# Encoder block on one core: the scan's 32x32 inversion split by column parity, its transfers merged and reordered, and the softmax weights computed ahead of the last row's norm

## The reference

```
def step(state, inp):
    r_t, w_t, k_t, v_t, kk_t, a_t = inp
    sa = einsum('zbhvk,zbhk->zbhv', state, -kk_t)
    state = (state * w_t[..., None, :] + sa[..., :, None] * (kk_t * a_t)[..., None, :]
             + v_t[..., :, None] * k_t[..., None, :])
    y = einsum('zbhvk,zbhk->zbhv', state, r_t)
...
kk = to_heads(k_raw * k_k);  kk = kk / max(sqrt(sum(kk * kk)), L2_EPS)
alpha = jax.nn.softmax(jnp.stack(lses), axis=0)        # weights of the three attention groups
o_attn = jnp.sum(alpha[..., None] * jnp.stack(outs), axis=0)
```

## Time and profile before

| | |
|---|---|
| median of 3 runs | 3364.0 us (3359.9 to 3370.8) |
| the profiled execution | 3362.9 us, span 3361.1 us |
| PE busy | 3258.0 us (97%) |
| DVE, ACT, POOL busy | 1852.6, 1310.0, 1580.3 us |
| projection / scan / output, from the span's start | 0 to 901.7 / to about 1600 / to 3361.1 us |

### The profile page before, as it was taken

How to read it: one execution, slowest core, us unless ns; L and a number is a source line. 1 busy time by engine, 2 the same in 40 slices (tenths; PEclk the granted TensorE clock), 3 DMA queues, 4 the chain that set the end, 5 groups by cost and what they waited for, 6 DMA issues and landing times.

```text
span 3361.1 us, 42103 instructions
## 1 busy us (share of the span) xinstructions
PE 3258.0 (97%) x15943; PEld 2692.0 (80%) x15943; DVE 1852.6 (55%) x2360; ACT 1310.0 (39%) x2139; POOL 1580.3 (47%) x1492
## 2 busy tenths in 40 slices
PE   7999999999889999999899999999999999999998
PEld 6788887777578888888588878888888888888886
DVE  3666565666667676772531034455455455455556
ACT  4544345554255665662442232223233233223222
POOL 4544443334278888885564443323323323323323
PEclk9999999999899999999899999999999999999999
DMA  5444454443455555552633323323323323323323
GB/s 171 122 151 138 141 154 132 129 120 103 114 137 143 129 130 141 146 135 82 242 115 136 113 69 113 107 88 107 112 83 109 111 81 117 103 84 117 107 82 106
DMA packets 666051, 405.06 MB, mean 121 GB/s; under 512 B 193534, under 2 KB 597178, under 8 KB 665338
## 3 DMA queue, kind: packets, MB, share of 16 engines
q1 hardware_dynamic: 665850, 402.38, 41.1%
HBM read 347.05 MB, written 54.53 MB: 119 GB/s over the span
## 4 chain that ended last, share of the span: by engine, by line
PE 50%; DVE 1%; ACT 0%; issue 0%; POOL 0%; DMA 0%; SPq 0%; DVEq 0%; ACTq 0%; POOLq 0%
PE f_bank L2207 9%; PE f_bank L2209 9%; PE f_bank L2208 9%; PE f_bank L2245 4%; PE f_bank L2247 4%; PE f_bank L2246 4%; PE f_bank L2185 2%; PE f_bank L2186 2%; PE f_bank L2187 2%; PE f_bank L2128 1%; PE f_bank L2129 1%; PE f_bank L2130 1%; PE f_bank L2163 0%; DMA orw_plain<-oat 0%; DVE orw_plain L2701 0%
## 5 line engine op out<-in xcount | busy, mean ns | idle before, releaser
L2496 POOL TENSOR_TENSOR w_lo_b<-w_raw_b,w_hi_b 128x1024 fp32r<-128x1024 f32 x176 | 435.9, 2479 | 903.4 <-ACT w_hi_b L2372 898.1
L2207 PE MATMUL f_bank<-act_rounded,w_lo_b 128*128 128x512 f32 x1408 | 549.2, 390 | 1.2 <-DVE act_rounded L2608 1.2
L2209 PE MATMUL f_bank<-act_rounded,w_hi_b 128*128 128x512 f32 x1408 | 547.8, 389 | 0.0
L2208 PE MATMUL f_bank<-act_rounded,w_hi_b 128*128 128x512 f32 x1408 | 547.8, 389 | 0.0
L1295 POOL TENSOR_TENSOR ring_w_rounded<-ring_w_plain,ring_w_hi 128x1024 fp32r<-128x1024 f32 x134 | 330.3, 2470 | 427.5 <-ACT ring_w_hi L1311 427.5
L1635 PE MATMUL slab_ps<-h_hi,ring_w_rounded 128*128 128x512 f32 x1056 | 426.4, 404 | 2.8 <-DVE h_lo L1462 2.4
L1636 PE MATMUL slab_ps<-h_lo,ring_w_hi 128*128 128x512 f32 x1056 | 414.9, 393 | 0.0
L1637 PE MATMUL slab_ps<-h_hi,ring_w_hi 128*128 128x512 f32 x1056 | 414.2, 392 | 0.0
L2372 ACT CAST w_hi_b<-w_raw_b 128x1024 fp32r<-128x1024 f32 x176 | 185.1, 1053 | 449.6 <-DMA w_raw_b<-in_w_ffn_up_dram 203.9
L2207 PEld LDWEIGHTS f_bank<-act_rounded,w_lo_b 128*128 128x128 f32 x1408 | 264.5, 188 | 55.7 <-DVE act_rounded L2608 1.1
L2209 PEld LDWEIGHTS f_bank<-act_rounded,w_hi_b 128*128 128x128 f32 x1408 | 264.3, 188 | 55.2
(11 more groups left out here) (434 smaller groups left out, 6176.9 us busy)
## 6 DMA issues: line engine op xcount, KB each, us to landing
ring_w_plain<-in_w_in_dram SPq DMA_DIRECT2D x190, 512.0 KB, 4.1
w_raw_b<-in_w_ffn_gate_dram SPq DMA_DIRECT2D x88, 512.0 KB, 3.6
w_raw_b<-in_w_ffn_up_dram SPq DMA_DIRECT2D x88, 512.0 KB, 3.6
w_raw_b<-in_w_ffn_down_dram SPq DMA_DIRECT2D x42, 512.0 KB, 3.9
w_raw_b<-in_w_out_dram SPq DMA_DIRECT2D x16, 1024.0 KB, 5.0
zt<-slab_out SPq DMA_DIRECT2D x63, 256.0 KB, 4.3
hid_plain<-in_w_ffn_down_dram SPq DMA_DIRECT2D x21, 512.0 KB, 4.2
oa_plain<-in_w_ffn_down_dram SPq DMA_DIRECT2D x21, 512.0 KB, 3.8
```

The lines of the kernel that those rows point to most:

```text
L2207: pe.matmul(o, wl[:, k, :], act_hi[:, kk, :], start=kk == 0, stop=False)
L2208: pe.matmul(o, wh[:, k, :], act_lo[:, kk, :], start=False, stop=False)
L2209: return pe.matmul(o, wh[:, k, :], act_hi[:, kk, :], start=False, stop=stop)
L2496: pool.tensor_tensor(low(r), slab_raw(j % 2), high(r).bitcast(F32), ALU.subtract).then_inc(slab_low, 1)
```

## The change

- *Inversion.* The inverse is no longer made in place but in a second tile, inv, of half the columns: each block goes to two partitions, 32 apart, and partition group r holds the columns of the inverse with parity r. Rows and columns of n on the side of a are stored with the even ones first and then the odd ones ("placed", "in_blocks"), so that POOL's operations still have regular strides. There are 31 steps of two operations, with 2k x n elements on 64 partitions. Three small masks are built at the start of the scan for the permuted orders.
- *ab and ak become abk.* Products with 64 rows of contraction, for each head of a group by itself, into two banks; no block-diagonal b_bd and k_bd, so ACT's "bd" goes. a comes to PE by way of var, and ACT negates it in "at". DVE masks in four stages' worth of 64-partition operations: "n" (the part that is stored) ahead of "ab" and "ak".
- *Transfers.* zt's rows are laid out so that six loads of a unit become two, and five of a bonus two. yb leaves in two stores, one for each parity, and blocks come in four loads of twice the partitions.
- *SP's order.* In odd slots the wait for the inversion and the yb stores stand first, then the n store, d_bd and low of the next unit, then the loads of blocks. d_bd and low of the other unit move to the next slot.
- *Projection.* "unit" of the last row moves from step TAIL + 2, ahead of "share", to step TAIL + 3, behind the first six "weigh"; its store moves with it.

```diff
-PE_SLOT = (("x1", "u"), ("ab", "v"), ("lx", "u"), ("ak", "v"), ("x3", "u"), ("av", "v"), ("qg", "u"),
+PE_SLOT = (("x1", "u"), ("abk", "v"), ("lx", "u"), ("x3", "u"), ("av", "v"), ("qg", "u"),
-DVE_SLOT = (("ab", "v"), ("xadd", "u"), ("ak", "v"), ("decays", "w"), ...
+DVE_SLOT = (("n", "v"), ("xadd", "u"), ("ab", "v"), ("ak", "v"), ("decays", "w"), ...
...
                 for it in range(NUNIT // 2):
-                    m = blocks[it % 2]
-                    pool.wait_ge(n_landed[it % 2], 64 * (it // 2 + 1))
-                    for j in range(HALF - 2, 0, -1):
-                        n = HALF - 1 - j
-                        pool.tensor_tensor(st, m[:, 0:j, j:j + 1].broadcast_to(shape), m[:, j:j + 1, j + 1:HALF].broadcast_to(shape), ...
-                        pool.tensor_tensor(m[:, 0:j, j + 1:HALF], m[:, 0:j, j + 1:HALF], st, ALU.add).then_inc(inv_chain, 1)
+                    m, x, step = blocks[it % 2], inv[it % 2], steps[it % 2]
+                    if it >= 2:
+                        pool.wait_ge(inv_stored[it % 2], 32 * (it // 2))
+                    pool.memset(x[:, :, :], 0.0).then_inc(inv_chain, 1)
...
+                    pool.wait_ge(n_landed[it % 2], 64 * (it // 2 + 1))
+                    for j in range(HALF - 1, 0, -1):
+                        k, n, c, at = (j + 1) // 2, EVERY - j // 2, j // 2, (j % 2) * EVERY + j // 2
+                        shape = [CH, 2, k, n]
+                        pool.tensor_tensor(st, rows(m)[:, :, 0:k, at:at + 1].broadcast_to(shape),
+                                           x[:, at:at + 1, c:EVERY].unsqueeze(1).broadcast_to(shape), ALU.mult).then_inc(inv_chain, 1)
+                        pool.wait_ge(inv_chain, done + 1)
+                        pool.tensor_tensor(rows(x)[:, :, 0:k, c:EVERY], rows(x)[:, :, 0:k, c:EVERY], st, ALU.add).then_inc(inv_chain, 1)
...
+                    if slot % 2 == 0 and slot >= 0:
+                        blocks_back(slot + 1)
+                    paired = slot % 2 and 0 <= slot + 1 < NUNIT
+                    if paired:
+                        it = (slot + 1) // 2
+                        sp.wait_ge(inverted, it + 1)
+                        for r in range(2):
+                            sp.dma_start(yb[it % 2, :, :, r, :], inv[it % 2][r * HALF:(r + 1) * HALF, :, :]).then_inc(inv_stored[it % 2], 16)
                     if 0 <= v < NUNIT:
-                        it, s = divmod(v, 2)
-                        sp.wait_ge(taken_dve, DVE_AT["ab", v])
-                        sp.dma_start(nb[it % 4, s].rearrange("q p t -> p q t"), n_sb[:, :, :]).then_inc(n_stored, 16)
+                        sp.wait_ge(taken_dve, DVE_AT["n", v])
+                        sp.dma_start(nb[(v // 2) % 4, v % 2].rearrange("q p t -> p q t"), n_sb[:, :, :]).then_inc(n_stored, 16)
+                    if paired:
+                        sp.wait_ge(inv_stored[it % 2], 32 * (it // 2 + 1))
+                        blocks_back(slot + 1)
+                    if 0 <= v < NUNIT and v % 2:
+                        it = v // 2
+                        sp.wait_ge(n_stored, 16 * (v + 1))
...
+                                sp.dma_start(blocks[it % 2][at:at + 16, :, :],
+                                             src[:, hb * HALF:(hb + 1) * HALF, hb * HALF:(hb + 1) * HALF]).then_inc(n_landed[it % 2], 16)
...
-                    elif name == "ab":
-                        pe.wait_ge(taken_act, ACT_AT["bd", n])
+                    elif name == "abk":
+                        pe.wait_ge(taken_dve, DVE_AT["operands", n])
                         for q in Q:
-                            ins = pe.matmul(bank[1][:, q, :], b_bd[:, q, :], xar[st][:, q, CH:3 * CH], start=True, stop=True)
+                            for e in range(2):
+                                r = slice(CH * e, CH * e + CH)
+                                ins = pe.matmul(bank[1 + 2 * e][:, q, :], bk[r, q, :], var[r, q, CH:3 * CH], start=True, stop=True)
...
-    if s - 2 in NORMS:
+    if s - 2 in NORMS and s != TAIL + 2:
         stages.append(("unit", s - 2))
...
+    if s == TAIL + 3:
+        stages.append(("unit", TAIL))
```

More of the change, by code:

```diff
@@ L56 @@
 HALF = 32
+EVERY = HALF // 2
 PARAMS = {}
@@ L459, in store_gate, with blocks_back @@
                         sp.dma_start(zt[row:row + P, :], gate[c % 2][:, :]).then_inc(gate_stored[c % 2], 16)
-                def bonus_rows(b, row):
-                    return zt[row + (b // 2) * P:row + (b // 2 + 1) * P, (b % 2) * HS:(b % 2 + 1) * HS]
+                def blocks_back(n):
+                    it, s = divmod(n, 2)
+                    if n >= 2:
+                        sp.wait_ge(made, PE_AT["x3", n - 2])
+                    else:
+                        sp.wait_ge(zeroed, N_ZERO)
+                    for hb in range(2):
+                        first = 8 * (2 * hb + s)
+                        src = yb[it % 2].rearrange("b i r t -> b i (r t)")[first:first + 8].rearrange("(q e) i t -> e i q t", e=2)
+                        for e in range(2):
+                            at = CH * e + HALF * hb
+                            sp.dma_start(d_bd[s][at:at + HALF, :, at:at + HALF], src[e]).then_inc(d_landed[s], 16)
+                    for e in range(2):
+                        first, last = CH * e + HALF * s, CH * e + HALF * (1 - s)
+                        sp.dma_start(low[s][first:first + HALF, :, last:last + HALF],
+                                     nb[it % 4, s, :, first:first + HALF, last - CH * e:last - CH * e + HALF].rearrange("q i t -> i q t")
+                                     ).then_inc(d_landed[s], 16)
                 load(0)
@@ L862, in _ @@
                             at = tiles_after(slot, name)
-                        if name == "ak" and b is not None and left >= SOON:
+                        if name == "lx" and b is not None and left >= SOON:
                             sum_bonus(b, slot, c)
@@ L935, in slab_rows @@
     p -= (A0 - Q0) // 3
-    return COL_RKV + which * RW + p * P, ROW_RKV + which * RW + p * P
+    return COL_RKV + which * RW + p * P, row_in_half(ROW_RKV, which, p)
 def taking(x):
@@ L1260, in _ @@
                         store(s - 1)
-                    if s - 2 in NORMS and s - 2 >= A0:
-                        row = ROW_KK + ((s - 2 - A0) // 3) * P
-                        sp.wait_ge(taken_dve, DVE_DONE["unit", s - 2])
+                    x = {TAIL + 2: None, TAIL + 4: TAIL}.get(s, s - 2)
+                    if x in NORMS and x >= A0:
+                        row = row_in_half(ROW_RKV, 3, (x - A0) // 3)
+                        sp.wait_ge(taken_dve, DVE_DONE["unit", x])
                         sp.dma_start(zt[row:row + P, :], kk_out[:, :]).then_inc(kk_stored, 16)
```

219 lines of the change are left out of this document (113 added, 106 removed).

## The result

The changed kernel is slower: 3407.3 us, the median of 4 runs (3405.4 to 3411.9), against 3362.0 of the kernel before on the same chip (3357.5 to 3370.8); the ratio is 1.0132, with an interval of 1.0115 to 1.0148. The forecast was 3378 us and the range 3324 to 3400, so the direction was forecast and the size was not. The profiled execution took 3406.5 us (span 3404.8), 43.6 more than that of before; the forecast was 15.8 more.

A forecast was written before the change was run, and what follows sets the result against it. It took POOL's inversion plus a hand-over through SP's queue to bound the scan: 31.0 + 10.1 = 41.1 us a pair. Then 3362.9 + 28.6 - 1 - 11.8 gave 3378 us; range 3324 to 3400.

The forecast's parts named there:

- The inversion: POOL's inversion in the scan: 31.0 us after the change against 39.0 measured before, from a line through operation prices.
- The hand-over: Inversion's end to POOL's next start: yb stores 3.5, issuing d_bd and low 2.7, loads of blocks 3.9; 10.1 us.
- The rival of small pieces: Hand-over: 64-byte yb writes cost 4.5 us or more and doubled blocks 1.5; period 42.8, 3404 us; chance 10%.
- They carry twice the bytes: 0 to 1.5 us more, I take 0.4: Last step of the hand-over: doubled loads of blocks add 0.4 us to 3.5 from issue to POOL's start.
- The scan's end: First inversion, fifteen periods of 41.1 us, then 7.6 to x1 of slot 30: 28.6 us later than before.
- The end of the projection: Last row's norm moved behind the softmax weights: -8.8 of wait, -4.2 of clock, +1.2 on DVE; -11.8 us.
- the 4.2 us of low clock: Loss to the lower clock behind PE's wait at the first spread, 865 to 875; counted as saved too.
- The rest: The two slots left behind x1 of slot 30: 0.9 us shorter, counted as -1.
- The 0.7 at most: PE in the scan: most that abk saves a slot against ab and ak, 0.35 x 2; 0.45 taken.
- PE paces the scan: Rival: inversion and hand-over together under 36.7 us, so waits of x1 go; 3313 or about 3328 us; chance 12%.
- 0.47: Chance of the forecast case: the scan's period 40.1 to 42.2 us, time 3363 to 3395.
- the two slower rivals: Scan: small pieces cost more, period 42.8, 3404 us, 10%; POOL not faster, period near 44, 3422 us, 5%.

The follow-up runs named there:

- Experiment 2: Kernel before with only SP's order changed: n store and loads of blocks behind the wait for the old inversion, blocks also behind d_bd and low; 3529.8 us, ratio 1.0494.
- experiment 1: Changed kernel with the n store and loads of blocks put back ahead of SP's wait for the inversion; 3321.8 us, ratio 0.9880; run again 3320.6 us, 0.9870.
- experiment 4: Changed kernel with the loads of d_bd and low moved behind the loads of blocks, wait for the inversion still first; 3370.8 us, ratio 1.0022 to the kernel before.
- experiment 5: Changed kernel with blocks loaded once, in four loads of 32 KB instead of 64 KB, half of each inverse left out; 3384.2 us, ratio 1.0063 to before.
- experiment 6: Kernel of experiment 1 without the reciprocal in the softmax weights' chain; 3323.4 us, ratio 0.9881 to the kernel before, against 0.9870 with the reciprocal.

## Why the prediction went as it did

**The mechanism was right.** SP's wait for the inversion ahead of POOL's next input makes a loop of inversion and hand-over, and that loop sets the pace. Experiment 2 shows it without the new inversion, experiment 1 takes it away, experiments 4 and 5 shorten it.

**The inversion**: 31.0 us forecast, 31.3 measured. The line through one short form and one long one held for operations on twice the partitions. The first inversion took 34.6 us where 33.2 were taken.

**The hand-over**: 3.5 + 2.7 + 3.9 = 10.1 forecast, 3.3 + 2.8 + 5.0 = 11.2 measured (means of 15). The first two terms held. SP went on 1.3 us later behind the yb store than before (3.3 for 2.0), and 0.95 of that is the issue of two DMAs (1.27 us) for one (0.32), so at most some 0.4 us is left for the pieces of 64 bytes; no run tried the pieces by themselves. The rival of small pieces was thus too high there: its 4.5 us was the landing of the n store in the kernel before, and the same store lands in 2.3 us in the changed kernel. The rule beside it, the least size of 512 bytes for line rate in the Trainium skill, "DMA: Bandwidth & Descriptors", Specifications, would make the pieces cost something; these rows agree in sign and leave it little.

The step that failed is the last: "They carry twice the bytes: 0 to 1.5 us more, I take 0.4". It is 1.2 us (experiment 5 against the changed kernel, by the hand-overs and by the period). The bound held, but the value taken was near nothing, without a row for a doubled transfer. The other 0.3 us come from the 3.5 for the single copy, read from one row; experiments 2 and 5 give 3.7 to 3.8 in the mean. Together 5.0 instead of 3.9, in each of 15 trips. In experiment 4, with other loads behind them, the doubled loads took 4.8. The rival of the small pieces named a period of 42.8, near the measured one, but its own prices (4.5 and 1.5 more for the blocks) sum to 43.2, and the stores did not cost that; its number came near by luck.

**The scan's end.** Counted from the start of the scan (901.72 before, 894.55 after), the first inversion started 0.6 us later than forecast and took 1.4 longer. From its end to the end of the last, each of the 15 periods was 42.5 us instead of 41.1: 20.5 us in all, of which the loads of blocks are 15 x 1.1 = 17 and the inversions 15 x 0.3 = 4. x1 of slot 30 stood 7.2 us behind the issue of yb instead of 7.6. Together 22.1 us over the forecast. (The 42.75 us of above is counted between starts and has the long first inversion in it.)

**The end of the projection**: -11.8 us forecast, -7.2 in the trace (901.72 to 894.55). "They are ready 8.8 us earlier, and PE waits 2.9" failed: it waits 5.05. The chain was moved into a stretch where POOL works through two 128x1024 operations, and two of its additions of 0.68 us took 2.8. The prediction carried the durations of the old place to the new one. The same POOL operations had before lain beside the norm (one product of the norm took 2.77 us there) and the head of the chain (3.46 us for two, 1.38 now). In sum: 4.2 us more for the two additions, 0.8 for a pair of products, 2.1 less at the head, so 2.9. The reciprocals, with one input, took 3.34 us beside POOL and alone. The Trainium skill, "SBUF — State Buffer", section "SBUF: two separate sides", says that a DVE operation with two inputs in SBUF and a GpSimd operation exclude each other for the whole instruction, whichever starts first; the additions of 2.8 us agree with it, and by it the prediction should have looked at POOL's timeline there. No run moved the POOL operations away, so this cause is read from the two timelines and not tried. The second half, that the 4.2 us of low clock go as well, failed too: behind a wait of 5.0 us the clock was still low. It would have failed in part with the wait that was forecast: in experiment 6, behind 3.05 us, the clock still fell for one spread, 1.4 us lost of the 4.2. The row that the prediction leaned on said so, since x1 at 1.32 us behind a wait of 3.3 is not the 1.05 of the high clock.

**The rest** was 0.2 us longer behind slot 30, not 1 shorter. Summed: 15.8 + 22.1 + 4.6 + 1.2 = 43.7, within rounding, the difference of the two profiled executions.

**PE's own work.** From the start of abk to that of the next product there are 1.09 us:

```profile
1210.69 1.16 PE L837 MATMUL sbank<-var,bk 64*128 64x128 f32 x16
1211.78 0.50 PE L816 MATMUL gbank<-h_hi,ring_w_rounded 128*128 128x512 f32 x1
```

For ab they were 0.82 (1200.72 to 1201.54), and as much for ak: 0.55 us saved a slot, where 0.45 was taken. The 0.7 at most of the prediction compared durations; by starts the eight records of the scores take 0.65 us (535.93 to 536.58), which would save only 2 x (0.82 - 0.65) = 0.34. An estimate from these rows: what does not grow with the number of records is 2 x 0.65 - 1.09 = 0.21 us. A drain at the two changes of the tiling mode, as the Trainium skill has it in "TensorEngine Tiling (Array Packing)", Key Properties, has to fit into that; no run here shows it by itself. The saving is hidden behind the loop in the changed kernel. In experiment 1, with PE in the lead, a slot takes 18.2 us ((1549.11 - 984.91) / 31, x3 of slot 0 to that of slot 31), 36.4 a pair; the forecast for PE was 36.7, and experiment 1 measured the time of the rival "PE paces the scan", 3313 to 3328. Its condition is not met, though: inversion and hand-over are no shorter, they only no longer stand one behind the other.

**The chances.** Slower had 0.48 and came true (three quarters of 0.47 and the two slower rivals would be 0.50). The range ended at 3400, and 3407 was measured. The loads of blocks alone would not have gone past it (3378 + 17 = 3395), nor all 15 periods (3378 + 20.5 = 3398.5); the 4.6 us at the end of the projection and the rest did. The range was also too narrow for its own bounds: the upper end of the hand-over (12.2) gives a period of 43.2, and the range held 42.6.

## What to carry to other kernels

In a queue that is served in order, put nothing that feeds an engine behind a wait for that same engine: here it turned 1.3% of gain into 1.3% of loss. A shorter operation repaired only part of it, since the inversion lost 8 us and the hand-over added 11. A term that stands inside a loop is multiplied by its trips, so its bounds have to reach the range. When a chain is moved to another time, look up what the neighbouring engines do there, because its durations belong to the old place. And a stage that comes back 15 times should be read as the mean of its 15 rows: here one cycle against another gave 1.6 us for a cost that is 1.2.

## What the runs showed of the hardware

- DVE's additions on 8 partitions by 512 took 0.68 us alone and 2.8 us beside a POOL subtraction of 128x1024 (5.40 us for two). An operation of DVE with one input in the same stretch (RECIPROCAL, 3.34 us) was not longer.
- The same kernel kept PE's low clock for different times behind the same wait. In the two executions of experiment 1 the wait was 5.04 us in both; the spreads ran 4.0 us apart until the third in the one and until the sixth in the other, 5.3 us of difference to the last spread. Mean granted clock of 860 to 870 and 870 to 880 in the first and in the second execution (columns as in the earlier trace rows):

```profile
860.00:870.00 10.00, 10.00 (x26) 5.96 (x25) 3.52 (x6) 1.04 (x1) 2.38 (x1) 0.65 0.31 79
870.00:880.00 10.00, 10.00 (x38) 6.19 (x38) 7.04 (x7) 1.05 (x1) 2.38 (x1) 1.00 0.35 104
```

```profile
860.00:870.00 10.00, 10.00 (x22) 6.19 (x22) 3.69 (x5) 1.04 (x1) 2.36 (x1) 0.50 0.37 105
870.00:880.00 10.00, 10.00 (x29) 5.97 (x28) 4.58 (x5) 1.05 (x1) 1.88 (x1) 0.71 0.12 29
```

  So a few microseconds of a clock dip can't be forecast from one execution here; the wait itself was the same in both.
- Stores of 64 KB in 64-byte pieces land in 2.6 us (median of 28), and let SP go on 3.3 us after the issue of two, 0.95 of the 1.3 us over the old store being the issue itself. Small pieces cost far less here than their number suggests.
- Loads of blocks in pieces of 128 bytes, four DMAs: 3.7 to 3.8 us from the first issue to POOL's start for 4 x 32 KB, 4.8 to 5.0 for 4 x 64 KB (means of 15 in experiments 2, 5, 4 and the changed kernel).
